# w_down as seven products of 512x512 weight sums, interleaved with w_up, in a one-core hybrid decoder layer

## The chip, the core and the metric

The kernel runs on one core of a Trainium2 chip. The metric is the device time of one execution in microseconds (us), and the figure for the kernel before is the median of three runs. The engines are named as the profile names them: PE (TensorE, matrix products), PEld (its weight loads), DVE (VectorE), ACT (ScalarE), POOL (GpSimd) and SP (SyncE, which here only issues transfers).

## What is computed

One layer on 256 tokens of width 2048, everything in 32-bit floats. The change lies in the last two lines of the layer, with w_up of 2048x8192 and w_down of 8192x2048:

```
h    = RMSNorm(x)
proj = h @ w_in                       # 2048 x 4096, then short convolution, pooling
x    = x + concat(y_conv, y_pool) @ w_out
h    = RMSNorm(x)
u    = relu(h @ w_up)
x    = x + (u * u) @ w_down
out  = RMSNorm(x)
```

## The kernel before

**Products in three parts.** PE multiplies 32-bit numbers here in a reduced form (fp32r). Each operand is split into that form (hi) and what is left of it (lo), and a product is hi·hi + hi·lo + lo·hi. For weights, ACT writes `w_hi` from `w_raw` (L449) and DVE writes `w_lo` = `w_raw` - `w_hi` (L628). For activations the same is done once, and hi and lo lie side by side.

**The stream of weights.** Weights come in chunks of 1 MB, [128 partitions, 4 x 512]: 512 rows by 512 columns of a weight matrix. Four chunks (2048 x 512) are a block. `w_raw`, `w_hi` and `w_lo` have four slots each, one per chunk of a block. SP issues the loads in one order (L197, `load_chunk`) and waits before each until DVE has read the slot four chunks earlier. ACT's `split` waits for the load and until PE has used the slot's previous chunk (`chunk_used`); DVE's `split` waits for ACT. All engines take their instructions strictly in the order written.

**Blocks.** There are 8 blocks of w_in, 4 of w_out, and then four parts p of 4 blocks of w_up and 4 blocks of w_down. Part p of w_up makes 2048 columns of u, and the part's w_down blocks take them up as 2048 rows. Banks of the accumulator (`ps`, 8 banks of 512 columns) are used in two sets of four, in turns.

- An up block (`gemm_block`) makes the transposed values: the weights are stationary, 64 pairs of a matmul of 512 columns (activation hi and lo beside each other, L252) and one of 256 columns (L255). Then ACT copies the one half of the banks to `cross` (L455), DVE adds the other half (`add_halves`, L635), scales by the token's norm (L664), and makes relu and square in one instruction (L891); ACT and DVE split the result into `act_b` (L477, L671).
- A down block (`row_block`, `row_products`, L343) has the activations stationary and the weights moving: 4 chunks x 4 x 3 x 2 token halves = 96 matmuls of 512 columns. DVE adds the two banks to `x` (`add_rows`, L649).

**The end.** The last block runs its two token halves one after the other; while the second runs, the first is normalised; then the second is added (L927), squared and scaled, and stored.

Of the kernel before, what the change touches and what calls it, by code (L numbers as in the profile page):

```python
# [47 lines left out]


def build(nc, x_t, x_rows, w_stream, pool_w, params, g_final, out):  # L50
# [4 lines left out]
    with ctx:  # L55
# [194 lines left out]
        def _(pe):  # L250
# [154 lines left out]
            gemm_block(FIRST_UP + 2, act_a, 0)  # L405
            gemm_block(FIRST_UP + 3, act_a, 1)

            def up_pair(n):
                gemm_block(n, act_a, 0)
                gemm_block(n + 1, act_a, 1)  # L410

            def down_pair(n, acts_before):
                row_block(n, 0, acts_before)
                row_block(n + 1, 1, acts_before)

            with pe.Fori(0, 2) as i:
                down_pair(2 * i + (FIRST_UP + 4), 8)
            with pe.Fori(1, PARTS - 1) as p:
                with pe.Fori(0, 2) as i:
                    up_pair(2 * i + PART_BLOCKS * p + FIRST_UP)  # L420
                with pe.Fori(0, 2) as i:
                    down_pair(2 * i + PART_BLOCKS * p + (FIRST_UP + 4), 4 * p + 8)
# [566 lines left out]
```

## Time and profile before

| | us |
|---|---|
| runs, median of 3 (lowest to highest) | 1001.91 (1000.73 to 1002.18) |
| the profiled execution | 1000.99 |
| its span, first to last instruction | 999.2 |
| PE busy | 986.5 (99%) |
| DVE busy | 586.4 (59%) |
| ACT busy | 419.6 (42%) |
| mean granted TensorE clock | 0.996 |

All durations below are from the one profiled execution. "Span" leaves out 1.8 us of that execution's own time. PE's busy time contains overlaps of pipelined matmuls, so that the pitch from one matmul to the next is read from the chain of waits and not from the duration of one.

### The profile page before, as it was taken

What the parts mean: (1) busy time and instruction counts of PE and PEld (TensorE: products, weight loads), DVE (VectorE), ACT (ScalarE), POOL (GpSimd) and SP (SyncE); (2) the same over time, 40 slices, a digit from 0 to 9 for tenths busy, and PEclk for the clock granted to TensorE, in tenths of its full rate; (3) what the DMA queues carried; (4) which work ended last, traced back from release to release, by engine and by line L of the source; (5) the groups of instructions that cost most, each with busy time, mean ns of one, the idle gap of its engine ahead of it and who ended that gap; (6) DMA issues with size and microseconds to landing.
All of it is one profiled execution on the core that took longest, in us unless ns stands there. A gap on an engine that the chain in (4) does not pass through costs nothing.

```text
span 999.2 us, 12457 instructions
## 1 busy us (share of the span) xinstructions
PE 986.5 (99%) x5088; PEld 847.2 (85%) x5088; DVE 586.4 (59%) x428; ACT 419.6 (42%) x325; POOL 1.4 (0%) x9
## 2 busy tenths in 40 slices
PE   8999999999999999999999999999999999999996
PEld 7888888888888888888888888888888888888885
DVE  6597777655554766544656654556565445656453
ACT  6644435354443434333444433343433334444342
POOL 0000000000000000000000000000000000000000
PEclk9999999999999999999999999999999999999998
DMA  9956543555544655555455455545545554555512
GB/s 327 392 194 229 190 188 122 215 211 190 189 169 169 233 189 195 183 208 177 165 211 206 176 203 191 187 151 213 209 183 207 176 204 132 211 209 205 187 66 84
DMA packets 29694, 193.52 MB, mean 194 GB/s; under 512 B 3296, under 2 KB 3552, under 8 KB 7136
## 3 DMA queue, kind: packets, MB, share of 16 engines
q1 hardware_dynamic: 29232, 190.85, 52.1%
q10 hardware_dynamic: 288, 1.18, 0.3%
q0 software_dynamic: 144, 1.05, 0.3%
q8 instruction: 24, 0.39, 0.2%
q14 instruction: 6, 0.05, 0.0%
HBM read 190.97 MB, written 2.10 MB: 193 GB/s over the span
## 4 chain that ended last, share of the span: by engine, by line
PE 94%; DMA 3%; SPq 1%; DVE 1%; ACT 0%; issue 0%; ACTq 0%
PE ps L343 44%; PE ps L252 33%; PE ps L255 17%; DMA w_raw<-w_stream 3%; SPq L208 1%; PE ps L277 0%; PE ps L329 0%; SPq L193 0%; DVE w_lo L628 0%; ACT w_hi L449 0%; PE ps L317 0%; DVE val L635 0%; PE ps L276 0%; PE ps L279 0%; ACT cross L483 0%
## 5 line engine op out<-in xcount | busy, mean ns | idle before, releaser
L628 DVE TENSOR_TENSOR w_lo<-w_raw,w_hi 128x2048 fp32r<-128x2048 f32 x172 | 392.0, 2291 | 280.4 <-ACT w_hi L449 279.7
L449 ACT ACTIVATE w_hi<-w_raw 128x2048 fp32r<-128x2048 f32 x172 | 326.8, 1912 | 344.0 <-PE ps L343 210.8
L252 PE MATMUL ps<-act_a,w_hi 128*128 128x512 f32 x1472 | 351.1, 391 | 0.0
L343 PE MATMUL ps<-w_hi,act_b 128*128 128x512 f32 x1280 | 345.3, 390 | 0.0
L252 PEld LDWEIGHTS ps<-act_a,w_hi 128*128 128x128 f32 x1472 | 271.0, 188 | 52.5
L343 PEld LDWEIGHTS ps<-w_hi,act_b 128*128 128x128 f32 x1280 | 239.8, 188 | 49.3
L343 PE MATMUL ps<-w_lo,act_b 128*128 128x512 f32 x640 | 199.7, 389 | 0.0
L255 PEld LDWEIGHTS ps<-act_a,w_lo 128*128 128x128 f32 x1472 | 188.6, 191 | 7.0
L255 PE MATMUL ps<-act_a,w_lo 128*128 128x256 f32 x1472 | 191.1, 283 | 0.0
L343 PEld LDWEIGHTS ps<-w_lo,act_b 128*128 128x128 f32 x640 | 120.2, 188 | 25.0
L635 DVE TENSOR_TENSOR val<-ps,cross 128x1024 f32<-128x1024 f32 x26 | 31.8, 1223 | 47.2 <-ACT cross L455 47.2
L455 ACT ACTIVATE cross<-ps 128x1024 f32<-128x1024 f32 x26 | 26.6, 1024 | 76.4 <-PE ps L255 74.6
L477 ACT ACTIVATE act_b<-val 128x1024 fp32r<-128x1024 f32 x18 | 19.1, 1060 | 67.4 <-DVE val L891 59.8
L649 DVE TENSOR_TENSOR x<-ps,x 128x1024 f32<-128x1024 f32 x19 | 23.3, 1224 | 22.4 <-PE ps L343 22.4
L671 DVE TENSOR_TENSOR act_b<-val,act_b 128x1024 fp32r<-128x1024 f32 x18 | 22.1, 1226 | 21.5 <-ACT act_b L477 21.5
L277 PE MATMUL ps<-act_a,w_hi 128*128 128x512 f32 x64 | 23.9, 414 | 2.0 <-DVE w_lo L723 2.0
L664 DVE TENSOR_TENSOR val<-val,inv_rms 128x1024 f32<-128x1024 f32 x18 | 22.0, 1225 | 5.3 <-ACT inv_rms L498 4.7
L483 ACT ACTIVATE cross<-x 128x512 f32<-128x512 f32 x16 | 9.9, 622 | 32.0 <-DVE x L649 18.9
L891 DVE SCALAR_TENSOR_TENSOR val<-val 128x1024 f32<-128x1024 f32 x16 | 19.6, 1226 | 0.6
L279 PE MATMUL ps<-act_a,w_lo 128*128 128x256 f32 x60 | 17.4, 290 | 0.0
L277 PEld LDWEIGHTS ps<-act_a,w_hi 128*128 128x128 f32 x64 | 12.6, 196 | 5.5 <-DVE w_lo L723 2.7
L723 DVE TENSOR_TENSOR w_lo<-w_raw,w_hi 128x512 fp32r<-128x512 f32 x16 | 11.0, 687 | 2.3 <-ACT w_hi L510 2.0
(68 smaller groups left out, 164.3 us busy)
## 6 DMA issues: line engine op xcount, KB each, us to landing
w_raw<-w_stream SPq DMA_DIRECT2D x172, 1024.0 KB, 4.8
w_raw<-w_stream SPq DMA_DIRECT2D x16, 256.0 KB, 7.9
x<-x_rows SPq DMA_DIRECT2D x2, 1024.0 KB, 17.4
mix_mem<-x_t SPq DMA_DIRECT2D x3, 512.0 KB, 8.2
out<-x SPq DMA_DIRECT2D x6, 256.0 KB, 2.7
mix_mem<-pool_w ACTq DMA_DIRECT2D x1, 1024.0 KB, 9.1
mix_mem<-g_final POOLq DMA_DIRECT2D x1, 1024.0 KB, 5.0
out<-val SPq DMA_DIRECT2D x2, 256.0 KB, 2.1
```

Source lines behind the costliest of these rows:

```text
L252: return pe.matmul(ps[:, bank, :], weights_hi, act, start=first, stop=False)
L255: return pe.matmul(ps[:, bank, 0:S], weights_lo, act[:, 0:S], start=False, stop=last)
L277: mm = pe.matmul(ps[:, bank, :], weights_hi, act, start=first, stop=last)
L343: mm = pe.matmul(ps[:, NT * parity + t, :], a[:, at:at + P], cols, start=first and i == 0, stop=last and i == 2)
L449: act.activation(w_hi[:, c, :], w_raw[:, c, :], ACT.Copy).then_inc(hi_ready, 1)
L455: act.activation(cross[:, :, :], bank_halves(parity, 1), ACT.Copy).then_inc(cross_ready, 1)
L628: dve.tensor_tensor(out=w_lo[:, c, :], in0=w_raw[:, c, :], in1=w_hi[:, c, :].bitcast(F32), op=ALU.subtract)\
L635: dve.tensor_tensor(out=val[:, :, :], in0=bank_halves(parity, 0), in1=cross[:, :, :], op=ALU.add).then_inc(summed, 1)
L649: dve.tensor_tensor(out=x_cols(j), in0=row_banks(parity), in1=x_cols(j), op=ALU.add)\
L664: dve.tensor_tensor(out=to, in0=val[:, :, :], in1=by_token(), op=ALU.mult)\
L671: dve.tensor_tensor(out=lo(act_b, k0, k0 + NT), in0=val[:, :, :], in1=hi(act_b, k0, k0 + NT).bitcast(F32), op=ALU.subtract)\
L891: dve.scalar_tensor_tensor(out=val[:, :, :], in0=val[:, :, :], scalar=0.0, in1=val[:, :, :], op0=ALU.max, op1=ALU.mult)\
```

## The change

The 16 up blocks (UPS) stay, one per 512 columns of u. w_down is cut anew: 8 slices (SLICES) of 1024 rows, each in two column halves of 1024, which makes 16 units. A unit is a product of a 256 x 1024 piece A of u·u with a 1024 x 1024 piece B of w_down, each seen as 2 x 2 quadrants (A: token half by 512 columns; B: 512x512, one chunk each).

For 14 units (SEVENS) the four quadrant products of two terms each, eight in all, are replaced by seven products with sums of quadrants (Winograd's variant of Strassen's form). Weight sums: T1 = B11+B12, T2 = T1+B22, T3 = B12+B22, T4 = T2+B21. T1 is made by DVE (a 128x2048 add). T2, T3 and T4 are each made by a transfer that POOL issues with `accum_op=add`, 1 MB from DRAM onto the chunk that lies in the on-chip buffer. The activation sums (S5, N6, N3, S7) are made by DVE on [128, 4, 128] pieces (`made`). Every product goes to one accumulator bank by 12 matmuls of 512 columns (`term`), and DVE adds or subtracts the banks into `x` seven times per unit in instructions of 512 columns (`fold`), reading a bank while it still accumulates for later terms. The two last units are done in the plain way, 8 chunks of 24 matmuls (`plain`).

One unit d is interleaved with one up block t = d+2, in 11 steps: up chunk 0, A11·B11, S5·T1, up chunk 1, N3·B22, N6·T2, up chunk 2, S7·T3, up chunk 3, A12·B21, A22·T4. Two up blocks (LEAD) run ahead. Up blocks always use banks 0 to 3, terms banks 4 to 6. Relu and norm are one DVE instruction (`add_up`) and the square moves to ACT (`square_up`). `w_hi` and `w_lo` keep their four slots, now filled in turn by step number; `w_raw` slots 0 and 1 are for w_up, 2 and 3 for B quadrants, and two more buffers (`sums`, in `mix_mem`) hold T1, T2, T4.

```diff
-            with sp.Fori(2, BLOCKS) as n:
+            with sp.Fori(2, FIRST_UP + LEAD) as n:
                 for c in range(CHUNKS):
                     load_chunk(n, c)
...
+            for t in range(LEAD, UPS):            # SP
+                d = t - LEAD
+                lead = d == 0
+                load_quad(sums[d % 2], d, 1, up_item(1, 0) if d < 2 else term_item(d - 2, A22_T4),
+                          sum_base_loaded[d % 2])
+                load_up(t, 0, up_item(1, 0) if lead else up_item(t - 1, 2))
+                load_quad(w_raw[:, 3, :], d, 3, up_item(1, 3) if lead else term_item(d - 1, S7_T3),
+                          raw_loaded[3])
+                load_up(t, 1, up_item(1, 1) if lead else up_item(t - 1, 3))
+                load_quad(w_raw[:, 2, :], d, 0, up_item(1, 2) if lead else term_item(d - 1, A12_B21),
+                          raw_loaded[2])
+                load_up(t, 2, up_item(t, 0))
+                load_quad(w_raw[:, 2, :], d, 2, term_item(d, A11_B11), raw_loaded[2])
+                load_up(t, 3, up_item(t, 1))
...
+            def add_quad(to, d, n, after, added):        # POOL
+                pool.wait_ge(lo_ready, after + 1)
+                pool.dma_start(to, w_quads[4 * d + n, :, :], accum_op=ALU.add).then_inc(added, 16)
+            for d in range(SEVENS):
+                add_quad(sums[d % 2], d, 3, term_item(d, S5_T1), t2_added)
+                add_quad(w_raw[:, 3, :], d, 1, term_item(d, N3_B22), t3_added)
+                add_quad(sums[d % 2], d, 2, term_item(d, N6_T2), t4_added)
...
+            for t in range(LEAD, UPS):                   # PE
+                d = t - LEAD
+                up_chunk(t, 0)                           # waits: summed by add_up(t - 1)
+                if d == 0:
+                    pe.wait_ge(summed, turn(FIRST_UP) + LEAD)
+                else:
+                    pe.wait_ge(folded, FOLDS * d)
+                term(d, A11_B11, A11, NT, True)
+                term(d, S5_T1, S5, NT + 1, True)
+                up_chunk(t, 1)
+                pe.wait_ge(folded, FOLDS * d + 2)
+                term(d, N3_B22, N3, NT + 1, False)
+                term(d, N6_T2, N6, NT, False)
+                up_chunk(t, 2)
+                pe.wait_ge(folded, FOLDS * d + 4)
+                term(d, S7_T3, S7, NT, False)
+                up_chunk(t, 3)
+                term(d, A12_B21, A12, NT + 2, True)
+                pe.wait_ge(folded, FOLDS * d + 5)
+                term(d, A22_T4, A22, NT, False)
+            pe.wait_ge(quad_ready, quad_count(last_slice, A21))
+            pe.wait_ge(folded, FOLDS * SEVENS - 1)
+            plain(0, range(HALVES), True)
+            pe.wait_ge(folded, FOLDS * SEVENS)
+            plain(1, range(HALVES), True)
...
+            def hi_of(g, raw):                           # ACT
+                act.wait_ge(chunk_used, g - 3)
+                act.activation(w_hi[:, g % 4, :], raw, ACT.Copy).then_inc(hi_ready, 1)
...
+                act.wait_ge(t2_added, 16 * (d + 1))
+                hi_of(term_item(d, N6_T2), sums[d % 2])
...
+                elif not folding:
+                    quad_hi(s + 1, A21, held[:, :, P:S], A22_T4)   # unit 13: waits for its last term
+            plain_hi(0)
+            take_up(UPS - 1)
+            plain_hi(1)
+            square_up(UPS - 1)
...
+            for t in range(LEAD, UPS):                   # DVE, in this order
+                d, s = t - LEAD, (t - LEAD) // 2
+                folding = d % 2 == 0
+                if d:
+                    fold(d - 1, 5, S7_T3, NT, 1, 1, ALU.subtract)
+                if folding:
+                    quad_lo(s, S7, part_2)
+                up_lo(t, 0)
+                add_up(t - 1)
...
+                dve.tensor_tensor(out=sums[d % 2], in0=sums[d % 2], in1=w_raw[:, 2, :], op=ALU.add)\
+                   .then_inc(t1_added, 1)
+                lo_of(term_item(d, A11_B11), w_raw[:, 2, :])
+                dve.wait_ge(squared, t)
+                if folding:
+                    made(... part_0 ...)                 # S5
+                if d:
+                    fold(d - 1, 6, A12_B21, NT + 2, 0, 0, ALU.add)
+                lo_of(term_item(d, S5_T1), sums[d % 2])
+                if folding:
+                    quad_lo(s, S5, part_0)
+                    made(... part_1 ...)                 # N6
+                if d:
+                    fold(d - 1, 7, A22_T4, NT, 1, 0, ALU.add)
+                up_lo(t, 1)
+                if folding:
+                    quad_lo(s, N6, part_1)
+                    made(... part_0 ...)                 # N3
+                elif s + 1 < SLICES - 1:
+                    make_s7()
+                lo_of(term_item(d, N3_B22), w_raw[:, 3, :])
+                if folding:
+                    quad_lo(s, N3, part_0)
+                fold(d, 1, A11_B11, NT, 0, 0, ALU.add)
+                lo_of(term_item(d, N6_T2), sums[d % 2])
+                if folding:
+                    quad_lo(s, A12, val[:, :, 0:P])
+                    quad_lo(s, A22, val[:, :, P:S])
+                else:
+                    quad_lo(s + 1, A11, held[:, :, 0:P])
+                fold(d, 2, S5_T1, NT + 1, 1, 1, ALU.subtract)
+                up_lo(t, 2)
+                lo_of(term_item(d, S7_T3), w_raw[:, 3, :])
+                fold(d, 3, N3_B22, NT + 1, 0, 1, ALU.subtract)
+                up_lo(t, 3)
+                fold(d, 4, N6_T2, NT, 0, 1, ALU.subtract)
+                lo_of(term_item(d, A12_B21), w_raw[:, 2, :])
+                lo_of(term_item(d, A22_T4), sums[d % 2])
+            fold(SEVENS - 1, 5, S7_T3, NT, 1, 1, ALU.subtract)
+            quad_lo(last_slice, A21, held[:, :, P:S])
+            plain_lo(0)
+            add_up(UPS - 1)
+            plain_lo(1)
+            fold(SEVENS - 1, 6, A12_B21, NT + 2, 0, 0, ALU.add)
...
```

`lo_of(g, raw)` waits for `hi_ready` and makes the 128x2048 `w_lo` of step g. `quad_lo` waits for ACT's half of an activation piece, makes the lo part in 512 columns, and waits for its own end; `made` is one 512-column DVE instruction and a wait for its end. `take_up` (ACT) and `add_up` (DVE, an add and the relu-and-norm) stand for L455, L635 and L664/L891. The comments in the diff are added here.

## Rows read from the trace of the kernel before

**Rows 1.** The page's first part: span and busy time by engine.

```profile
span 999.2 us, 12457 instructions
PE 986.5 (99%) x5088; PEld 847.2 (85%) x5088; DVE 586.4 (59%) x428; ACT 419.6 (42%) x325; POOL 1.4 (0%) x9
```

**Rows 2.** The page's chain that ended last: share of the span by line.

```profile
PE ps L343 44%; PE ps L252 33%; PE ps L255 17%; DMA w_raw<-w_stream 3%; SPq L208 1%; PE ps L277 0%; PE ps L329 0%; SPq L193 0%; DVE w_lo L628 0%; ACT w_hi L449 0%; PE ps L317 0%; DVE val L635 0%; PE ps L276 0%; PE ps L279 0%; ACT cross L483 0%
```

**Rows 3.** The chain in order of time: start us, us, what.

```profile
285.28 3.63 PE ps L252 x16
...
551.77 87.07 PE ps L343 x384
638.84 3.63 PE ps L252 x16
...
727.87 87.07 PE ps L343 x384
```

**Rows 4.** Waits: engine line waited for, us in total, times, longest us.

```profile
DVE w_lo L628 <- ACT w_hi L449: 279.7, 134, 7.0
```

**Rows 5.** Groups by line and shape: count | busy, mean ns | idle before, releaser.

```profile
L628 DVE TENSOR_TENSOR w_lo<-w_raw,w_hi 128x2048 fp32r<-128x2048 f32 x172 | 392.0, 2291 | 280.4 <-ACT w_hi L449 279.7
L449 ACT ACTIVATE w_hi<-w_raw 128x2048 fp32r<-128x2048 f32 x172 | 326.8, 1912 | 344.0 <-PE ps L343 210.8 <-PE ps L255 129.0 <-DMA w_raw<-w_stream 4.1
L635 DVE TENSOR_TENSOR val<-ps,cross 128x1024 f32<-128x1024 f32 x26 | 31.8, 1223 | 47.2 <-ACT cross L455 47.2
L455 ACT ACTIVATE cross<-ps 128x1024 f32<-128x1024 f32 x26 | 26.6, 1024 | 76.4 <-PE ps L255 74.6 <-PE ps L277 1.8
L527 ACT ACTIVATE act_b<-win 128x512 fp32r<-128x512 f32 x4 | 2.5, 633 | 20.9 <-DVE win L760 20.9
L927 DVE TENSOR_TENSOR x<-ps,x 128x512 f32<-128x512 f32 x2 | 1.4, 690 | 10.1 <-PE ps L343 10.1
```

**Rows 6.** DVE in order of time: start us, us, what; the starts give the pitch.

```profile
103.14 1.23 DVE L664 TENSOR_TENSOR mix_mem<-val,inv_rms 128x1024 f32<-128x1024 f32 x1
104.40 1.22 DVE L809 TENSOR_TENSOR mix_mem<-mix_mem,inv_rms 128x1024 f32<-128x1024 f32 x1
105.55 2.29 DVE L628 TENSOR_TENSOR w_lo<-w_raw,w_hi 128x2048 fp32r<-128x2048 f32 x1
107.75 0.69 DVE L749 TENSOR_TENSOR win<-mix_mem 128x512 f32<-128x512 f32 x1
108.47 2.15 DVE L749 TENSOR_TENSOR win<-win 128x512 f32<-128x512 f32 x3
```

**Rows 7.** Busy time in two stretches: PE, PEld, DVE, ACT, POOL, PEclk, DMA share, GB/s.

```profile
639.00:727.00 88.00, 88.00 (x507) 77.74 (x506) 52.20 (x29) 36.21 (x22) 0.00 (x0) 1.00 0.51 190
12.00:41.00 29.00, 29.00 (x164) 25.37 (x164) 17.77 (x28) 21.14 (x32) 0.15 (x1) 1.00 1.03 415
```

**Rows 8.** Transfers: count, KB each, median us from issue to landing; POOL's one issue.

```profile
w_raw<-w_stream SPq DMA_DIRECT2D x172, 1024.0 KB, 4.8
x<-x_rows SPq DMA_DIRECT2D x2, 1024.0 KB, 17.4
mix_mem<-g_final POOLq DMA_DIRECT2D x1, 1024.0 KB, 5.0
...
200.58 0.65 POOL L246 DMA_DIRECT2D mix_mem<-g_final  x1 [146.98 <-DVE val L842]
```

**Rows 9.** Stretches of 1 us around two idle times of PE, columns as in rows 7.

```profile
6.00:7.00 1.00, 0.00 (x0) 0.00 (x0) 0.24 (x1) 0.63 (x1) 0.00 (x0) 1.00 0.84 200
...
8.00:9.00 1.00, 1.00 (x5) 0.90 (x4) 0.48 (x1) 0.15 (x2) 0.00 (x0) 0.50 0.98 361
...
10.00:11.00 1.00, 1.00 (x4) 0.57 (x3) 1.00 (x3) 1.00 (x3) 0.00 (x0) 0.50 1.01 397
...
991.00:992.00 1.00, 0.05 (x1) 0.00 (x0) 0.88 (x2) 0.19 (x1) 0.00 (x0) 1.00 0.00 0
...
994.00:995.00 1.00, 0.00 (x0) 0.00 (x0) 0.96 (x3) 0.86 (x2) 0.00 (x0) 0.54 0.00 0
```

More of the change, by code:

```diff
@@ L404, in _ @@
             pe.wait_ge(inv_rms_ready, 2)
[L405 to L422, printed above, removed]
@@ new lines, in plain @@
+            def plain(f, halves, done):
+                g = FIRST_PLAIN + f
+                d, k2, n = PLAIN_OF[f]
+                bank = (6, 4, 0, 2)[2 * d + n]
+                of_half = ((A11, A21), (A12, A22))[k2]
+                pe.wait_ge(hi_ready, g + 1)
+                pe.wait_ge(lo_ready, g + 1)
+                for k in range(CK):
+                    for i, (at, of) in enumerate(((0, w_hi), (P, w_hi), (0, w_lo))):
+                        for t in halves:
+                            mm = pe.matmul(ps[:, bank + t, :], quads[:, of_half[t], k, at:at + P],
+                                           weights_of(of, g, k), start=k2 == 0 and k == 0 and i == 0,
+                                           stop=k2 == 1 and k == CK - 1 and i == 2)
+                if done:
+                    mm.then_inc(chunk_used, 1)
+                return mm
@@ L440, in _ @@
+            plain(5, range(HALVES), True)
+            for t in range(HALVES):
+                plain(6, (t,), False)
+                plain(7, (t,), False).then_inc(half_done, 1)
         @block.scalar
@@ new lines, in plain_hi @@
+            def plain_hi(f):
+                slot, loads = plain_raw(f)
+                act.wait_ge(raw_loaded[slot], 16 * (loads + 1))
+                hi_of(FIRST_PLAIN + f, w_raw[:, slot, :])
+            plain_hi(0)
+            take_up(UPS - 1)
+            plain_hi(1)
+            square_up(UPS - 1)
+            act.wait_ge(squared, UPS)
+            quad_hi(SLICES - 1, A12, val[:, :, 0:P], A12_B21)
+            quad_hi(SLICES - 1, A22, val[:, :, P:S], A22_T4)
+            for f in range(2, PLAINS):
+                plain_hi(f)
@@ new lines, in _ @@
+            plain_lo(0)
+            add_up(UPS - 1)
+            plain_lo(1)
+            fold(SEVENS - 1, 6, A12_B21, NT + 2, 0, 0, ALU.add)
+            dve.wait_ge(squared, UPS)
+            quad_lo(last_slice, A12, val[:, :, 0:P])
+            quad_lo(last_slice, A22, val[:, :, P:S])
+            plain_lo(2)
+            fold(SEVENS - 1, 7, A22_T4, NT, 1, 0, ALU.add)
+            plain_lo(3)
+            plain_lo(4)
+            plain_lo(5)
+            dve.wait_ge(folded, FOLDS * SEVENS)
```

312 lines of the change are left out of this document (244 added, 68 removed).

## The prediction

> **What bounds the kernel now.** The page's head comes first: PE is busy for 986.5 of 999.2 us, DVE for 586.4, ACT for 419.6 [rows 1]. The chain that ended last shows whether that is work or overlap: L343, L252 and L255 hold 94% of the span, transfers 3% [rows 2]. In order of time the chain has whole blocks without a gap: 384 matmuls of L343 in 87.07 us, which is 0.2268 us each, and then up blocks from 638.84 to 727.87, which is 89.03 us for 16 chunks, 5.56 each [rows 3]. The waits say the same from the other side: DVE's longest total is for ACT (279.7 us), and ACT in its turn waits for slots that PE frees [rows 4, 5]. In a stretch of up blocks DVE is busy for 52.2 of 88 us at a clock of 1.00 and a DMA share of 0.51 [rows 7]. PE is the bound and is fed in time; only fewer PE columns make the kernel faster, as long as DVE, whose work grows most, keeps up.
>
> **What goes from PE.** Eight quadrant products of 12 matmuls become seven in 14 units: 14 x 12 = 168 matmuls of 512 columns fewer, x 0.2268 = **-38.1 us** [rows 3]. A unit with its up block is then 4 x 5.56 + 7 x 2.72 = 41.3 us of PE, against 44.0 before.
>
> **What DVE gets, and where.** Prices by pitch (start to start) [rows 6]: a 128x2048 instruction 2.20 (105.55 to 107.75); 1024 columns 1.26 if the next waits for its end (103.14 to 104.40), else 1.15; 512 columns 0.72 with such a wait (107.75 to 108.47), else 0.62 (0.69 less the same overlap of 0.07). A fold is the shape of L927, 0.69 us [rows 5]. Per unit: 11 `lo_of` and T1, 12 x 2.20 = 26.4; `add_up` 2.4; 7 folds 4.3; in even units nine pieces of activation sums 6.5, in odd ones two, 1.4. That makes 39.6 us (even) and 34.5 (odd) out of 41.3. It fits as a sum, 90% busy, but DVE goes in one fixed order and PE waits in the middle of it, so the order decides.
>
> I follow one even unit from T, the moment PE ends S7·T3 of the unit before. Two things fix DVE's start: up chunk 3 ends at T+5.56, ACT's copy takes 1.02 [rows 5], so `add_up` begins at T+6.6 whatever DVE did before (until then it has lo A22·T4, a fold, a piece and lo of up chunk 0, done at about T+5). From there to the end of fold 2 stand: add and scale 2.41; six 128x2048 instructions (T1 and lo of A11·B11, S5·T1, up chunk 1, N3·B22, N6·T2) 13.2; three `made` and five `quad_lo` 5.76; folds 6, 7, 1 and 2 2.55. Sum 23.9, end T+30.6. PE may start N3·B22 only after fold 2 (`folded` 7d+2). Without waits it would be there at T + 3 x 5.56 + 4 x 2.72 = T+27.6. So PE stands for **3.0 us in each even unit**, even if no transfer is late. In an odd unit six pieces less give T+26.2, 1.3 us to spare. After fold 2 nothing is late: fold 4 ends at T+38.5, S7·T3 needs it at T+41.6. DVE's next start is fixed again by up chunk 3, so a period is the end of fold 2 plus 13.7 us of PE, and no stall is won back. ACT is no bound: 11 x 1.91 + 2 x 1.02 + at most 7 x 0.63 = 27.5 us of 41.
>
> **The accumulating transfer.** T2 is sent by POOL after lo of S5·T1 (T+17.1 even, T+16.4 odd). ACT's hi (1.91) and DVE's lo (2.29) of N6·T2, then two or one `quad_lo` and fold 2, stand behind its landing: fold 2 ends at T+23.4+L even, T+22.0+L odd, L from DVE's end to the landing. It hurts above L = 7.2 (even) and 5.6 (odd). The queue behind that waiting ACT instruction holds the activation pieces, up chunk 2 and S7·T3; behind DVE's lo stands the fold that PE waits for. No row shows an accumulating transfer. Lower bound: POOL's plain 1 MB, 5.0 us [rows 8]; upper: 17.4 us, a 1 MB load queued behind the first rush [rows 8]. I take L = 8.0: the issue 0.65, the plain landing 4.8 [rows 8], and once more the bytes, since the sum must read what it adds to: 1.05 MB at the 415 GB/s of the busiest stretch is 2.5 us [rows 7]. That lies nearer the row of 5.0, as these transfers meet one or two others and not a dozen. It gives a wait of 3.8 us in even units and 2.4 in odd ones. T3 (9 us until needed) and T4 (13 us) pass at that L. Were L 5.0, even units wait 3.0 and odd ones not at all; at 17.4 they wait 13.2 and 11.8.
>
> The Trainium skill (Collectives: The Full Stack, "The bandwidth ceiling: the fold count and why AG ≠ RS ≠ AR") says that a transfer with an add emits two source reads per chunk into the same ring, so that it delivers about half of a copy's rate. No row here shows it. By that rule the data part of L is doubled, which is my 8.0; by a copy's price L would be 5.5 and the sum 23 us lower.
>
> **The first unit** has no terms of a unit before it, so PE comes earlier. With E the end of the second up block, `add_up` starts at E+1.1; T1, two lo's, a `made` and `quad_lo` of S5 end at E+11.5, where PE wanted S5·T1 at E+8.3: 3.2 us. Then fold 2 ends at 10.9 + 8.0 + 6.3 = E+25.2 and PE is there at E+19.8: 5.4 us. Together 8.6 (7.2 at the low L).
>
> **The tail.** Activation piece A21 of the last slice waits on ACT for the last term of unit 13, although its slot holds nothing; call that moment X. ACT: piece to X+0.6, hi of plain 0 to X+2.5, copy of the last up block to X+3.5. DVE: lo of plain 0 from X+2.5, `add_up` (2.4), lo of plain 1, fold 6. PE's plain 0 waits for fold 6: 2.5 + 2.20 + 2.41 + 2.20 + 0.69 = **10.0 us** during which PE has nothing. After that plain 1 (5.44 us later) finds fold 7 done, and the end (L927 and on) is as before.
>
> **The clock.** PE was idle throughout 6 to 7 us; the granted clock was 0.50 (1.2 GHz) at 8 to 9 and still at 10 to 11 us. At the end PE stops 0.05 us after 991; the clock is 1.00 there and 0.54 at 994 to 995 [rows 9]. So a stop of some 3 us lets it fall, and three us at half speed cost 1.5. The tail and the first unit pay it: 3.0. The six other even stops of 3.8 us are just beyond 3: between 0 and 1.5 each, I take 0.75, the middle: 4.5. Odd units: none.
>
> **Sum.** -38.1 + 8.6 + 6 x 3.8 + 7 x 2.4 + 10.0 + 3.0 + 4.5 = +27.6. The profiled execution took 1000.99 us with its ends (span 999.2); 1000.99 + 27.6 = 1028.6. The median of the runs is 0.9 above the profiled one: **1029 us**. The likeliest case's own range, L from 6.5 to 9.5 and the clock at either bound, is 1008 to 1055.
>
> **Rivals.**
> 1. *The transfer costs what a plain one does* (L up to 5.6). Then only DVE's order binds: 7.2 + 6 x 3.0 + 10.0 = 35.2, clock 3.0 to 7.5: with -38.1 that is +0.1 to +4.6 on 1001.9, so 1002 to 1007. For it: POOL's plain transfer landed in 5.0 us. Against it: the buffer must be read too, and odd units send T2 only 2.8 us before two plain loads follow.
> 2. *Faster: the order has more slack than counted.* The place is fold 2 in even units. If DVE reaches it 3 us earlier (from which point the stop is gone) and L is below 5.6, only the first unit and the tail are left: -38.1 + 7.2 + 10.0 + 3.0 = -17.9, 984 us. For it: DVE's sum of 39.6 fits in 41.3. Against it: add_up's start hangs on PE's up chunk 3, and each instruction behind it is priced by its own pitch.
> 3. *Transfers crowd each other.* A unit moves 8 plain chunks and 3 accumulating ones; counted double that is 14.7 MB, 35 us at 415 GB/s in a period of 45, against a DMA share of 0.51 now [rows 7]. With L = 11, even units wait 6.8, odd ones 5.4, the first 11.6, and the clock falls in nearly all: -38.1 + 11.6 + 40.8 + 37.8 + 10.0 + 14 x 1.5 + 1.5 = +84.6, 1087 us. For it: the row of 17.4. Against it: the median of 4.8 with half the engines' time free.
> 4. *The change doesn't do what it says*, for instance if the matmuls of `term` come at another pitch than 0.2268. They have the operands' shapes of L343, so this gets little.
>
> **Chances.** Forecast 0.43, rival 1 0.17, rival 2 0.22, rival 3 0.15, rival 4 0.03. A measurement of this kernel can tell 0.2% (2 us) from no change. Faster: rival 2 and a little of 1, 0.25. Same: the low part of rival 1, 0.08. Slower 0.67. The range for 8 in 10 cuts rival 3 above a mean L of about 10, and half of rival 2: 984 to 1062.
>
> **What would show it.** Matmuls of 512 columns fewer by 168. In the middle of every even unit a gap of PE ahead of N3·B22, released by DVE's fold, of 3 to 4 us; in odd units one of about 2.4 behind `t2_added`. ACT's hi of N6·T2 waiting for the transfer; its landing near 7.3 us after the issue. A gap of 10 us after the last term, clock 0.5 behind it. DVE busy near 88%. The forecast is wrong if PE has no gaps in even units (then DVE's order was read wrong), if the landing is below 5 us, or if waits stand at up chunks, behind plain loads.

## The result: 1059.5 us, 5.9% slower

| | before | after | forecast |
|---|---|---|---|
| median of 4 runs each (lowest to highest), us | 1001.32 (1000.36 to 1002.18) | 1059.46 (1058.86 to 1062.32) | 1029 (984 to 1062) |
| ratio to before, 95% interval | 1 | 1.0587 (1.0564 to 1.0609) | |
| profiled execution / its span, us | 1000.99 / 999.2 | 1059.1 / 1057.2 | 1028.6 |
| mean granted TensorE clock | 0.996 | 0.966 | |

The direction was right, the size was not: +58.1 us between the profiled executions, +27.6 forecast. The page of after, first part, the chain by engine and the transfers (they answer to [rows 1, 2, 8]):

```profile
span 1057.2 us, 12002 instructions
PE 982.4 (93%) x4920; PEld 835.2 (79%) x4920; DVE 765.4 (72%) x619; ACT 525.9 (50%) x420; POOL 37.7 (4%) x51
...
PE 56%; DVE 18%; DMA 14%; issue 6%; ACT 4%; SPq 1%; ACTq 0%; DVEq 0%
...
w_raw<-w_quads SPq DMA_DIRECT2D x50, 1024.0 KB, 5.6
mix_mem<-w_quads POOLq DMA_DIRECT2D x28, 1024.0 KB, 10.1
...
w_raw<-w_quads POOLq DMA_DIRECT2D x14, 1024.0 KB, 11.2
```

PE has the 168 matmuls less. But where 94% of the chain of before was matmuls, PE now holds 56%, and DVE, transfers and ACT hold 36%: PE is fed too late. The two lines of POOL are the adding transfers: 10.1 us (T2 and T4) and 11.2 us (T3) from issue to landing.

**An odd unit**, the chain in order of time from the end of up chunk 3 on (start us, us, what; it answers to [rows 3]), and PE's own row (the bracket is the idle time before it and its releaser):

```profile
377.46 1.03 ACT cross L772
...
378.51 1.23 DVE win L1148
...
380.91 2.29 DVE mix_mem L1198
383.20 2.01 DVE w_lo L1138
...
386.00 2.21 DVE w_lo L1138
...
388.50 8.71 DMA mix_mem<-w_quads
...
397.23 1.93 ACT w_hi L758
...
401.39 0.69 DVE act_b L1157
402.10 0.70 DVE x L1167
...
402.85 0.50 PE ps L546
```

```profile
402.85 0.50 PE L546 MATMUL ps<-w_hi,act_b 128*128 128x512 f32 x1 [2.72 <-DVE x L1167]
```

Read it downwards: copy, `add_up`, T1 (L1198), lo of A11·B11, lo of S5·T1 (L1138), then POOL's T2, which lands 9.0 us after DVE's end (388.21 to 397.21), hi and lo of N6·T2, an activation piece, fold 2 (L1167), and PE starts N3·B22 2.72 us late. That is the chain which the prediction followed, link by link.

**The clock behind the stop.** Four stretches of 1 us behind that stop, columns as in [rows 7]:

```profile
403.00:404.00 1.00, 1.00 (x5) 0.83 (x6) 1.00 (x1) 0.00 (x0) 0.00 (x0) 1.00 0.97 262
404.00:405.00 1.00, 1.00 (x5) 0.76 (x4) 0.99 (x1) 0.00 (x0) 0.00 (x0) 0.61 1.06 270
405.00:406.00 1.00, 1.00 (x4) 0.81 (x3) 0.00 (x0) 0.00 (x0) 0.00 (x0) 0.50 0.81 197
406.00:407.00 1.00, 1.00 (x4) 0.71 (x4) 0.00 (x0) 0.41 (x1) 0.00 (x0) 0.50 1.30 262
```

The granted clock falls from 1.00 to 0.50 (2.4 to 1.2 GHz), 1.4 us after PE has restarted at 402.85, and matmuls of 512 columns start 0.43 us apart instead of 0.23 until it comes back.

**An even unit** ends by another chain, in order of time, and has a stop of its own (PE's row below it):

```profile
534.57 2.30 DVE w_lo L1138
...
537.16 10.19 DMA w_raw<-w_quads
...
547.37 1.93 ACT w_hi L758
...
549.35 2.17 issue
551.53 0.68 DVE x L1167
...
552.27 2.06 issue
554.33 0.69 DVE x L1167
...
555.06 0.50 PE ps L546
```

```profile
437.65 0.50 PE L546 MATMUL ps<-w_hi,act_b 128*128 128x512 f32 x1 [2.61 <-DVE x L1167]
```

T3 lands 10.2 us after its issue; hi, then DVE's lo of S7·T3 and of up chunk 3 (both "issue" here), with fold 3 between them and fold 4 behind, and PE gets S7·T3. The stop of 2.61 us stands ahead of A11·B11, where PE waits for `folded` 7d, fold 7 of the unit before; its odd-unit twin is 0.43 us.

**The balance.** Stops are PE's idle time in the trace; half clock is the sum of 1 minus the granted clock over stretches of 1 us in which it was below 0.95.

| | stops, us | half clock, us | sum | forecast |
|---|---|---|---|---|
| first unit | 0.63 + 2.33 + 4.53 = 7.5 | 3.4 | 10.9 | 8.6 + 1.5 |
| 6 even units, each | 2.61 + 0.64 = 3.25 | 1.7 | 4.95 | 3.8 + 0.75 |
| 7 odd units, each | 0.43 + 3.12 = 3.55 | 1.95 | 5.5 | 2.4 + 0 |
| tail | 10.15 | 2.8 | 12.95 | 10.0 + 1.5 |

All stops in the units sum to 51.9 us (forecast 8.6 + 22.8 + 16.8 = 48.2), the half clock in them to 27.2 (forecast 6.0). With -38.1 and both figures of the tail that is 54.0 of 58.1 us. In the tail the clock is at 0.50 when PE restarts at 1002.74 and stays there for 5.6 us, of which this stretch shows five:

```profile
1003.00:1008.00 5.00, 5.00 (x13) 3.89 (x12) 4.91 (x5) 2.71 (x2) 0.00 (x0) 0.50 0.77 234
```

The rest, 4.1 us, fits the way in which stops are counted. The up chunk ahead of the stop of 2.61 us runs from 429.34 to 437.65, 8.31 us where 5.54 is usual: a delay of 2.77, 0.16 more than the idle time, because the profile draws a matmul 0.39 us long when the next one starts after 0.23. For the 29 stops that makes about 4.6 us.

### The profile page after: what moved, and what is told of

Its sections match the earlier page's. It is cut to its first block, busy times and chain, and to the rows that moved or that the text cites. A ratio compares the mean times of both kernels' runs of the same rounds, so it can differ in the third digit from the quotient of the medians.

```text
span 1057.2 us, 12002 instructions
## 1 busy us (share of the span) xinstructions
PE 982.4 (93%) x4920; PEld 835.2 (79%) x4920; DVE 765.4 (72%) x619; ACT 525.9 (50%) x420; POOL 37.7 (4%) x51
## 4 chain that ended last, share of the span: by engine, by line
PE 56%; DVE 18%; DMA 14%; issue 6%; ACT 4%; SPq 1%; ACTq 0%; DVEq 0%
PE ps L364 20%; PE ps L367 11%; DVE w_lo L1138 8%; PE ps L455 8%; DMA mix_mem<-w_quads 8%; PE ps L588 4%; PE ps L546 4%; DMA w_raw<-w_quads 4%; PE ps L548 4%; PE ps L552 4%; ACT w_hi L758 3%; DVE mix_mem L1198 2%; DMA w_raw<-w_stream 2%; DVE x L1167 2%; ACT cross L772 1%
## 5 line engine op out<-in xcount | busy, mean ns | idle before, releaser
L364 PE MATMUL ps<-act_a,w_hi 128*128 128x512 f32 x1472 | 349.8, 390 | 0.0
L1138 DVE TENSOR_TENSOR w_lo<-w_raw,w_hi 128x2048 fp32r<-128x2048 f32 x120 | 274.3, 2287 | 60.6 <-ACT w_hi L758 59.4
L546 PE MATMUL ps<-w_hi,act_b 128*128 128x512 f32 x392 | 167.4, 427 | 51.3 <-DVE x L1167 48.9
L367 PE MATMUL ps<-act_a,w_lo 128*128 128x256 f32 x1472 | 191.0, 283 | 0.0
L548 PE MATMUL ps<-w_hi,act_b 128*128 128x512 f32 x392 | 164.3, 419 | 0.0
L758 ACT ACTIVATE w_hi<-mix_mem 128x2048 fp32r<-128x2048 f32 x42 | 80.6, 1918 | 123.5 <-DMA mix_mem<-w_quads 69.5
L1138 DVE TENSOR_TENSOR w_lo<-mix_mem,w_hi 128x2048 fp32r<-128x2048 f32 x42 | 96.1, 2288 | 60.5 <-ACT w_hi L758 60.3
L546 PEld LDWEIGHTS ps<-w_hi,act_b 128*128 128x128 f32 x392 | 79.8, 204 | 73.4 <-DVE x L1167 54.6
L552 PE MATMUL ps<-w_lo,act_b 128*128 128x512 f32 x392 | 110.6, 406 | 0.6 <-DVE w_lo L1138 0.6
L552 PEld LDWEIGHTS ps<-w_lo,act_b 128*128 128x128 f32 x392 | 78.4, 200 | 18.6 <-DVE w_lo L1138 1.1
L548 PEld LDWEIGHTS ps<-w_hi,act_b 128*128 128x128 f32 x392 | 80.0, 204 | 16.1
L455 PE MATMUL ps<-w_hi,act_b 128*128 128x512 f32 x256 | 68.8, 390 | 0.0
L1167 DVE TENSOR_TENSOR x<-x,ps 128x512 f32<-128x512 f32 x98 | 66.8, 681 | 1.1
L455 PEld LDWEIGHTS ps<-w_hi,act_b 128*128 128x128 f32 x256 | 47.8, 188 | 9.7
L351 POOL DMA_DIRECT2D mix_mem<-w_quads x28 | 24.3, 868 | 795.0 <-DVE w_lo L1138 795.0
L588 PE MATMUL ps<-w_hi,act_b 128*128 128x512 f32 x128 | 37.5, 407 | 10.2 <-DVE x L1167 10.2
## 6 DMA issues: line engine op xcount, KB each, us to landing
mix_mem<-w_quads POOLq DMA_DIRECT2D x28, 1024.0 KB, 10.1
mix_mem<-w_quads SPq DMA_DIRECT2D x14, 1024.0 KB, 12.9
w_raw<-w_quads POOLq DMA_DIRECT2D x14, 1024.0 KB, 11.2
```

Of the source, the lines that this page charges most:

```text
L364: return pe.matmul(ps[:, bank, :], weights_hi, act, start=first, stop=False)
L367: return pe.matmul(ps[:, bank, 0:S], weights_lo, act[:, 0:S], start=False, stop=last)
L455: mm = pe.matmul(ps[:, NT * parity + t, :], a[:, at:at + P], cols, start=first and i == 0, stop=last and i == 2)
L546: pe.matmul(to, quads[:, quad, k, 0:P], weights_of(w_hi, g, k), start=first and k == 0, stop=False, skip_group_check=not first)
L548: pe.matmul(to, quads[:, quad, k, P:2 * P], weights_of(w_hi, g, k), start=False, stop=False, skip_group_check=not first)
L552: mm = pe.matmul(to, quads[:, quad, k, 0:P], weights_of(w_lo, g, k), start=False, stop=k == CK - 1, skip_group_check=not first)
```

## The experiments

All ratios are to before, timed on the same chip (its medians there 1000.3 to 1000.8 us). Where an expectation names theories by letter, A is the late landing of the adding transfers (A1: by their own double reading), C the plain loads that they crowd. "Unit" is the time from one ACT copy of an up block to the next, even and odd as the parity of d.

### The adding transfer by itself

A small kernel in which POOL sends the same 1 MB transfer in four ways: copies one by one, adding ones one by one, four at once, and adding ones beside SP's plain loads.

> A small kernel that holds only transfers of 1 MB (128 x 2048 floats) from DRAM, issued by POOL, one after the other: six copies, six adding ones onto the same buffer, four copies at once, four adding ones at once, and six adding ones beside a stream of copies from SP. The rest of the layer is left out and the output is zeros. Theory A1 (an adding transfer moves its bytes twice): copies land in 5.0 to 5.6 us, adding ones in 7.5 to 8.1; four at once take about 12 and 22 us. Theory A2 (adding is slower than twice the bytes, whatever is beside it): adding ones land in 9 to 10 us alone. Beside the stream: over 10 us by either.

POOL in order of time (the bracket: idle before, and what it waited for):

```profile
22.89 0.53 POOL L26 DMA_DIRECT2D buf<-w  x1 [4.81 <-DMA buf<-w]
...
50.10 0.86 POOL L29 DMA_DIRECT2D buf<-w  x1 [7.40 <-DMA buf<-w]
58.34 0.85 POOL L29 DMA_DIRECT2D buf<-w  x1 [7.38 <-DMA buf<-w]
...
82.80 2.13 POOL L32 DMA_DIRECT2D buf<-w  x4 [7.39 <-DMA buf<-w]
95.91 3.57 POOL L36 DMA_DIRECT2D buf<-w  x4 [10.98 <-DMA buf<-w]
118.85 3.51 POOL L39 MEMSET zero<- 128x4096 f32 x1 [19.37 <-DMA buf<-w]
...
148.81 0.87 POOL L42 DMA_DIRECT2D buf<-w  x1 [12.08 <-DMA buf<-w]
161.01 0.86 POOL L42 DMA_DIRECT2D buf<-w  x1 [11.34 <-DMA buf<-w]
```

One after the other, a copy takes 5.34 us (17.55 to 22.89) and an adding transfer 8.24 (50.10 to 58.34). Four at once take 13.1 us as copies (82.80 to 95.91) and 22.9 as adding ones (95.91 to 118.85), 1.75 times as long. Beside a stream of plain loads one takes 12.2. So the estimate of 8.0 was right for a transfer alone, and wrong for one in company. The rule of the Trainium skill that the prediction weighed (Collectives: The Full Stack, "The bandwidth ceiling: the fold count and why AG ≠ RS ≠ AR"), a transfer with an add at about half a copy's rate, is what the group of four shows within an eighth.

### The transfers' price in the kernel

> POOL's three transfers of each unit are plain 1 MB copies instead of adding ones (T2, T3 and T4 are then not sums); every instruction, wait and order stays. Theory A (the landing of the adding transfer sets the end of 14 units, since it is longer than a copy's): in the changed kernel it landed 9.0 us (odd units) and 10.5 us (even units) after DVE's instruction; a copy should land in 5.5 to 6.5 us. Odd units then take about 41.5 to 42 us, even ones 45.4 us (fold order and the clock), so 14 units shrink from 657 to about 610 us and the kernel takes about 1012 us. Rival B (the order of DVE's instructions alone makes the time, the transfer lies beside it): over 1045 us.

```diff
-pool.dma_start(to, w_quads[4 * d + n, :, :], accum_op=ALU.add).then_inc(added, 16)
+pool.dma_start(to, w_quads[4 * d + n, :, :]).then_inc(added, 16)
```

1011.82 us (1010.91 to 1013.33), ratio 1.0110 (1.0094 to 1.0127). The transfers of its page:

```profile
mix_mem<-w_quads POOLq DMA_DIRECT2D x28, 1024.0 KB, 5.3
...
w_raw<-w_quads POOLq DMA_DIRECT2D x14, 1024.0 KB, 6.7
```

Without the add 48 of the 58 us are gone. The units are 42.0 to 42.4 us (odd) and 44.6 to 45.8 (even): the fold-2 stop is gone from both, which leaves 0.43 us in odd units, and in even ones the 2.61 ahead of A11·B11 with the clock behind it.

> POOL's three transfers of each unit are left out, and ACT doesn't wait for them (T2, T3, T4 are never formed). Theory A: only DVE's order, the first unit and the tail are left: 1005 to 1012 us, within 6 us of the run with plain copies. Rival C (crowding: the plain loads of SP are late because the adding transfers share the engines with them): clearly faster than the run with plain copies, by 10 us or more. Rival B: over 1045 us.

```diff
-add_quad(sums[d % 2], d, 3, term_item(d, S5_T1), t2_added)      # and those of T3 and T4
-act.wait_ge(t2_added, 16 * (d + 1))                             # and those for T3 and T4
```

1012.36 us (1011.89 to 1014.29), ratio 1.0117 (1.0100 to 1.0134). The same as with copies, so moving 42 MB more beside the loads costs nothing. In after itself, all 29 waits of ACT for a transfer in the units end with the landing of an adding one and none with a plain load; crowded plain loads are no cause there. The add's landing is.

### The order in which DVE meets a late landing

> Only DVE's order is changed: fold 2 goes ahead of lo of N6T2, folds 3 and 4 go ahead of lo of S7T3. PE waits for these folds, and they no longer stand behind an instruction that waits for an adding transfer. The transfers stay as they are. Theory A, second part (the landing costs time only because the folds stand behind it in DVE's order): PE needs hi of N6T2 at T+30 and has it at T+27, so odd units take 41.7 us and even ones 45.4 (the stop ahead of A11B11 and the clock remain): about 1012 us, as with plain copies. If PE itself waits for the sums (the landing is exposed in any order), the time stays above 1045 us.

```diff
 fold(d, 1, A11_B11, NT, 0, 0, ALU.add)
+fold(d, 2, S5_T1, NT + 1, 1, 1, ALU.subtract)
 lo_of(term_item(d, N6_T2), sums[d % 2])
...
+fold(d, 3, N3_B22, NT + 1, 0, 1, ALU.subtract)
+fold(d, 4, N6_T2, NT, 0, 1, ALU.subtract)
 lo_of(term_item(d, S7_T3), w_raw[:, 3, :])
-fold(d, 3, N3_B22, NT + 1, 0, 1, ALU.subtract)
 up_lo(t, 3)
-fold(d, 4, N6_T2, NT, 0, 1, ALU.subtract)
```

1023.98 us (1022.08 to 1028.14), ratio 1.0229 (1.0212 to 1.0246): 35 us back with the transfers still landing in 10.2 and 12.3 us. Odd units are 42.0 again; a landing of 10 us costs nothing there, and it cost 5 us only because folds that need no transfer stood behind a `lo_of` that waits for one. The time is 12 us above the expected 1012 all the same. Even units stay at 47.2 to 49.2, where 45.4 was expected: DVE still waits at lo of S7·T3, is late at fold 7, and the stop ahead of A11·B11 grows from 2.6 to between 4.0 and 4.8 us.

> Only fold 7 of the unit before is moved ahead of the first activation sum, so that the stop of 2.6 us ahead of A11B11 in even units goes. Theory A: no gain to speak of, since the chain through T3's transfer ends later than that stop: 1053 to 1060 us; the 2.6 us come back as a longer wait ahead of N3B22 or S7T3. Rival B (stops of DVE's order add up): 6 x 2.6 us and the clock less, 1035 to 1040 us.

```diff
+fold(d - 1, 6, A12_B21, NT + 2, 0, 0, ALU.add)
+fold(d - 1, 7, A22_T4, NT, 1, 0, ALU.add)
 made(... part_0 ...)                                  # S5
-fold(d - 1, 6, A12_B21, NT + 2, 0, 0, ALU.add)
 lo_of(term_item(d, S5_T1), sums[d % 2])
...
-fold(d - 1, 7, A22_T4, NT, 1, 0, ALU.add)
```

A miss: 1081.86 us (1079.78 to 1084.22), ratio 1.0807 (1.0789 to 1.0825), 22 us slower than after. PE in order of time:

```profile
453.07 0.80 PE L546 MATMUL ps<-w_hi,act_b 128*128 128x512 f32 x1 [5.48 <-DVE x L1167]
...
456.65 1.91 PE L552 MATMUL ps<-w_lo,act_b 128*128 128x512 f32 x4
```

The stop of 2.61 us is gone from A11·B11, but DVE's chain to fold 2 is no shorter: PE comes earlier and waits there in one piece (4.3 to 7.1 us in all units but the first). In the unit of these rows the clock is already at half in the first matmul after it (0.80 us) and stays there for 5.9 us, now behind the stop where it delays what follows. POOL's T2 goes out 0.8 us later, because fold 7 now stands ahead of lo of S5·T1. An early stop was cover for a late one.

> Only the end of the stretch is changed: ACT's piece A21 no longer waits for the last term of unit 13, and DVE does folds 6 and 7 of that unit ahead of lo of plain 1 and add_up. By the prediction's tail (10.0 us of waiting, measured 10.15, and half clock behind it) the kernel gets 10 to 11.7 us faster: 1047 to 1050 us. If the wait only moves to the next chunk of weights, under 5 us.

```diff
-quad_hi(s + 1, A21, held[:, :, P:S], A22_T4)
+quad_hi(s + 1, A21, held[:, :, P:S], None)            # no wait for the last term
...
 plain_lo(0)
-add_up(UPS - 1)
+fold(SEVENS - 1, 6, A12_B21, NT + 2, 0, 0, ALU.add)
+fold(SEVENS - 1, 7, A22_T4, NT, 1, 0, ALU.add)
 plain_lo(1)
-fold(SEVENS - 1, 6, A12_B21, NT + 2, 0, 0, ALU.add)
+add_up(UPS - 1)
```

1045.49 us (1044.24 to 1046.65), ratio 1.0443 (1.0425 to 1.0460), 14.0 less than after and 1.5 more than was expected at most. Between the profiled executions it is 12.5 (1059.1 and 1046.65): 9.1 of the stop, of which 1.07 us are left, and 2.8 of the clock behind it. The change removes this row of after, the forecast's tail of 10.0 us:

```profile
1002.74 1.20 PE L588 MATMUL ps<-w_hi,act_b 128*128 128x512 f32 x2 [10.15 <-DVE x L1167]
```

> The adding transfers stay as they are; the order on DVE is mended in all places that the traces point to: T1 is added ahead of add_up (in DVE's idle time), folds 6 and 7 follow lo of A11B11, fold 2 goes ahead of lo of N6T2, folds 3 and 4 ahead of lo of S7T3, and the tail as in the run of the tail alone. Theory A (latency exposed by order, not by bandwidth): PE waits only in the first unit and for DVE's work of 39.6 us now and then: 14 x 41.6 us, 970 to 985 us, faster than the kernel before. If DVE at 90% load can't keep up beside its waits for ACT and the transfers: 990 to 1005 us. If the engines that move data are the bound: over 1010 us.

The three orders above, and:

```diff
+dve.tensor_tensor(out=sums[d % 2], in0=sums[d % 2], in1=w_raw[:, 2, :], op=ALU.add)   # T1, with its waits
 add_up(t - 1)
-dve.tensor_tensor(out=sums[d % 2], in0=sums[d % 2], in1=w_raw[:, 2, :], op=ALU.add)
```

A miss again: 1022.29 us (1020.12 to 1026.15), ratio 1.0218 (1.0189 to 1.0246), where 970 to 985 was expected. DVE's row of T1, and the chain's row ahead of it:

```profile
508.96 2.29 DVE L1197 TENSOR_TENSOR mix_mem<-mix_mem,w_raw 128x2048 f32<-128x2048 f32 x1 [0.28 <-DMA w_raw<-w_quads]
```

```profile
502.19 6.74 DMA w_raw<-w_quads
```

B11 lands 6.74 us after lo of A12·B21 has let its slot go; T1 waits for it and takes 2.2 us, and `add_up`, which PE needs at up chunk 0, stands behind both (stops of 1.4 to 3.6 us there). The same orders without that move:

> As the run with all orders mended, but T1 is added behind add_up again, as in the changed kernel. There T1, moved ahead, waited for the load of B11 (6.7 to 8.4 us after lo of A12B21) and held add_up and so PE's next up chunk back by 1.4 to 3.6 us in each unit. Theory D (that wait took what the other orders gave): PE is not held at the up chunks any more, 14 x 2.4 us less 1 or 2: 992 to 1005 us. If the adding transfer of T3 (12 us) is the bound by itself: 1012 us or more.

1004.50 us (1002.87 to 1007.53), ratio 1.0046 (1.0030 to 1.0061), clock 0.994, just inside the expected 992 to 1005: 55 of the 58 us are given back by orders alone, and this still does not reach before. In this order ACT does wait for a plain load, too. In each unit but the first, its first hi (A11·B11) stands 2.8 to 4.8 us for the load of B11, for instance:

```profile
506.78 1.92 ACT L758 ACTIVATE w_hi<-w_raw 128x2048 fp32r<-128x2048 f32 x1 [3.21 <-DMA w_raw<-w_quads]
```

> The run with orders mended, without POOL's transfers and ACT's waits for them (T2, T3, T4 are never formed). What is left is PE's columns and the order of DVE: 14 x 41.5 to 42 us, first unit 3 to 4 us late: 968 to 978 us. It bounds what any faster way of making the weight sums could reach; if it stays above 990 us, DVE's load is what the mended orders lack and not the transfers.

```profile
span 966.2 us, 11938 instructions
PE 950.9 (98%) x4920; PEld 816.6 (85%) x4920; DVE 766.5 (79%) x619; ACT 527.5 (55%) x420; POOL 1.4 (0%) x9
```

968.14 us (967.55 to 969.20), ratio 0.9681 (0.9665 to 0.9697). With the same orders and no sums by transfer, every unit but the first (40.9) is 41.3 to 41.4 us, the forecast's 41.3 of PE. So DVE's load is no bound in a right order, and the adding transfers cost 36 us even then. How much of that is their own landing, and how much the loads of B11 that are late beside them, is not separated: plain copies were not run in this order.

### The clock

> PE does eight matmuls of 512 columns into an unused bank (1.8 us, their result is not read) at the places where it stops: ahead of the wait for fold 2 in odd units, and ahead of the wait before A11B11 in even units. Everything else is as in the changed kernel. If the half clock behind the stops is on the path in odd units (1.5 us each) it goes, since the remaining idle time is about 1 us: 7 x 1.5 = 10 us faster, 1048 us; in even units nothing is gained, as T3's transfer ends later. If the clock doesn't matter, 1058 to 1062 us.

```diff
+for _ in range(8):                        # odd units; in even ones ahead of the wait for 7d
+    pe.matmul(ps[:, 7, :], act_a[:, 0, 0:P], act_a[:, 1, :], start=True, stop=True)
 pe.wait_ge(folded, FOLDS * d + 2)
```

1051.86 us (1050.92 to 1055.07), ratio 1.0521 (1.0504 to 1.0539), 7.6 less than after. The half clock in the units shrinks from 27.2 to 6.7 us, so only a third of it came back. Odd units in which it no longer fell take 45.5 to 46.4 us, the two in which it did 47.9 and 48.0: there it is on the path. Even units hardly move (46.3 for 46.7), since T3's chain ends them whatever PE's clock does before: with fillers as without, S7·T3 starts within 0.2 us of the end of fold 4.

### Company of the transfers

> The changed kernel with the loads of w_up in the 14 units cut to 64 of 2048 columns (the rest of w_up is left out, old values are multiplied in its place); every instruction and wait stays. Theory A with crowding (the adding transfer takes 8.2 us alone and 9 to 12 beside other loads): T2 and T3 land in 8.3 to 9 us, 14 units get 1.0 to 1.5 us shorter each: 1036 to 1046 us. If the plain loads beside them don't matter: over 1055 us.

```diff
-sp.dma_start(w_raw[:, c % 2, :], w_stream[CHUNKS * (FIRST_UP + t) + c, :, :])
+sp.dma_start(w_raw[:, c % 2, 0:64], w_stream[CHUNKS * (FIRST_UP + t) + c, :, 0:64])
```

1046.61 us (1045.81 to 1047.75), ratio 1.0466 (1.0448 to 1.0483), 12.9 less than after, 0.6 above the upper end of what was expected. Odd units take 45.3 us for 47.1, even ones 46.5 for 46.7. Landings:

```profile
mix_mem<-w_quads POOLq DMA_DIRECT2D x28, 1024.0 KB, 8.6
...
w_raw<-w_quads POOLq DMA_DIRECT2D x14, 1024.0 KB, 10.3
```

> The changed kernel with the loads of w_up in the 14 units cut to 64 of 2048 columns and T4's transfer and its wait left out (both leave part of w_up and w_down out of the result), order and everything else kept, so that the adding transfers of T2 and T3 have nearly no company. Landing then 8.2 to 8.6 us for both, as in the run of transfers alone. Theory A with its parts sized: odd units 16.4 + 8.5 + 5.6 + 13.7 and 1.5 for the clock = 45.6 us; even ones 45.4 by DVE's order and the clock behind the stop ahead of A11B11: 1034 to 1042 us, which leaves about 8 to 12 us over the forecast of 1029 for the clock in odd units. If it falls to 1029 or below, crowding was the whole of what the forecast missed.

The same without T4: 1045.17 us (1041.73 to 1047.68), ratio 1.0444 (1.0415 to 1.0472).

```profile
mix_mem<-w_quads POOLq DMA_DIRECT2D x14, 1024.0 KB, 8.1
...
w_raw<-w_quads POOLq DMA_DIRECT2D x14, 1024.0 KB, 10.1
```

T2 lands as in the small kernel, and the first odd unit, in which the clock stays at 1.00, takes 44.3 us (forecast 43.7); from the next one on the clock falls and odd units take 46.2 on average. T3's median stays at 10.1 us, but it still has company: SP's 1 MB load of the base of a later T1 (B12 into `mix_mem`), issued some 3 us before it. In even units the two are in flight together for 3.4 to 4.5 us and T3 takes 8.5 to 10.2, in odd ones for 5.8 to 8.5 us and it takes 10.4 to 11.6. Unit 13 has no such load. T3's issues in units 11 and 13:

```profile
w_raw<-w_quads POOLq DMA_DIRECT2D x1, 1024.0 KB, 10.4
...
w_raw<-w_quads POOLq DMA_DIRECT2D x1, 1024.0 KB, 8.1
```

The run before has 8.2 us in unit 13, too. That points to this load; no run leaves it out alone.

> As the run before in this list, and POOL waits for the landing of T3's transfer before it issues T4's. T3's and T4's adding transfers were in flight together (issues 4 us apart), and T3, which is needed first, landed after 12 us. Theory E (the adding transfers crowd each other): T3 lands in 9.5 to 10.5 us and the kernel gets 5 to 15 us faster than without this. Against it: T4 lands later and may hold hi of A22T4: no gain, or a loss.

On top of the mended orders:

```diff
+pool.wait_ge(t3_added, 16 * (d + 1))
 add_quad(sums[d % 2], d, 2, term_item(d, N6_T2), t4_added)
```

1046.14 us (1042.75 to 1046.25), ratio 1.0447 (1.0428 to 1.0465), 42 slower than the orders alone. POOL's wait (us in total, times, longest):

```profile
POOL mix_mem L351 <- DMA w_raw<-w_quads: 161.8, 14, 12.5
```

POOL's queue is in order too: T4 and the next T2 leave late. T3 still landed in 12.2 us, so T4 was not what slowed it.

### Looking for a version that beats before

Five more kernels move the sums about within the mended orders. N3·B22's operands first, T3 so being sent earlier, with T4 still later (it inherits that fault):

> As the run with T4 later, and in even units hi and lo of N3B22 go ahead of the activation sums N6 and N3 on ACT and DVE, so that T3's transfer is issued 2.1 us earlier. If T3's transfer is the end of a unit's chain, even units get up to 2 us shorter: 6 to 14 us faster than without. If DVE's load of 39.6 us is the bound: no difference beyond 2 us. Best guess 985 to 998 us, below the kernel before.

1049.39 us (1043.86 to 1051.84), ratio 1.0483 (1.0445 to 1.0521). Without it:

> The run with orders mended (T1 behind add_up, all sums by transfer, 1004.5 us) with N3B22 ahead in even units. The same reasoning: 992 to 998 us if T3's transfer ends even units there.

```diff
-quad_hi(s, N6, part_1, N6_T2)
 hi_of(term_item(d, N3_B22), w_raw[:, 3, :])
+quad_hi(s, N6, part_1, N6_T2)                         # DVE: lo of N3·B22 ahead of made(N6)
```

1002.56 us (1000.70 to 1004.95), ratio 1.0023 (1.0013 to 1.0033). T2 by a DVE add of the size of T1's, in all units, and in odd ones only:

> The run with orders mended (T1 behind add_up), and T2 = T1 + B22 is added by DVE right after lo of S5T1 in all units (2.2 us more of DVE each: 41.8 us in even units, 36.7 in odd ones), so that POOL only issues T3 and T4. Theory F (in that run the serial chain of T2's and T4's transfers on one buffer ends odd units, and T3's even ones): odd units near 41.6 us, even ones 43 to 45: 985 to 998 us. If DVE's load is the bound: 14 x (39.3 + waits), over 1003 us.

> The same with T2 added by DVE in odd units only, by a transfer in even ones. Theory F: odd units near 41.6 us, even ones as in the run with orders mended (44): 985 to 993 us, faster than with T2 by DVE in all units by 0 to 10 us, since DVE's 2.2 us ahead of lo of N3B22 delay T3's transfer there. If both are equal, T3's transfer is no longer what ends even units.

```diff
-add_quad(sums[d % 2], d, 3, term_item(d, S5_T1), t2_added)
...
 lo_of(term_item(d, S5_T1), sums[d % 2])
+dve.tensor_tensor(out=sums[d % 2], in0=sums[d % 2], in1=w_raw[:, 3, :], op=ALU.add).then_inc(t2_by_dve, 1)
```

1008.24 us (1007.23 to 1009.28), ratio 1.0079 (1.0062 to 1.0096), and 1001.62 us (1000.00 to 1004.27), ratio 1.0011 (1.0002 to 1.0021). In the first, odd units are 41.3 to 43.2 but even ones 46.0 to 47.1. There the added instruction stands between lo of S5·T1 and lo of the piece S5, and PE stops 2.7 us ahead of S5·T1 (0.5 with all sums by transfer):

```profile
522.18 0.57 PE L546 MATMUL ps<-w_hi,act_b 128*128 128x512 f32 x1 [2.69 <-DVE act_b L1157]
```

A place behind that piece was not tried. N3 first with T2 by DVE in odd units:

> The run with T2 by DVE in odd units, and in even units hi and lo of N3B22 go ahead of the activation sums N6 and N3, so that T3's transfer is issued 2.1 us earlier. In the run before even units took 45.0 us and odd ones 43.0, with PE waiting for hi of S7T3 in even units. If T3's transfer ends even units: 43 us instead of 45, 986 to 993 us, the first version below the kernel before. If DVE's work does: within 3 us of 1002.

1000.75 us (997.56 to 1003.04), ratio 1.0003 (0.9993 to 1.0013). All five best guesses were too low, the first by 51 us, the others by 5 to 10; two times fit the other branch that was named, DVE's load or work as the bound (over 1003 with T2 by DVE in all units, within 3 us of 1002 in the last). Even the last has units of 42.3 to 45.0 us behind the first, not 41.3. PE stops in its even units 1.2, 0.5 and 0.9 us, each time for DVE, and transfers still hold 26% of its chain; which of the two binds is not separated. The best of them equals before; none that forms all the sums beats it.

## Why the prediction went wrong, point by point

The direction and the chain were right; what failed is mainly one term, the clock. The forecast was 30.5 us short (+58.1 against +27.6). Half clock in the units was 27.2 us where 6.0 was forecast, and 13.6 of these 21 us lie in the odd units, where the term stood at nothing.

- **What goes from PE: right.** 168 matmuls fewer, and 41.3 us for a unit that waits for nothing.
- **DVE's load: right.** 39.6 and 34.6 us per unit, as forecast (39.6, 34.5). Two unit stretches of after, columns as in [rows 7]:

```profile
422.10:469.10 47.00, 43.48 (x214) 36.71 (x213) 39.61 (x30) 25.43 (x18) 2.58 (x3) 0.96 0.81 246
469.10:515.50 46.40, 43.43 (x215) 36.75 (x214) 34.62 (x25) 23.67 (x15) 2.59 (x3) 0.96 0.82 249
```

- **The clock: this term failed.** The forecast gave even stops 0.75 us each and odd ones none, because it took "a stop of some 3 us" as the point from which the clock falls. Behind nearly all stops of 2.5 to 2.9 us it fell too, for 1.7 us of PE time each. The tail's clock was 2.8 for 1.5. In odd units it lies on the path (3.4 us per unit missed: about 1.9 of it clock); in even units most of it is cover for T3's chain, as the filled stops showed.
- **L: right alone, too low in company.** 8.2 us by itself; in the kernel, from DVE's end and on average, 8.5 for T2 in even units, 9.4 in odd ones, and 11.0 for T3 in even units. Without most of the company (no T4, small loads of w_up) odd units take 1.3 us less (45.86 for 47.13), some of it clock, and even ones 0.7 less (45.96 for 46.69).
- **"T3 passes": failed.** It ends every even unit. Hi, two lo's and two folds stand between its landing and PE, and T3 can't be sent before lo of N3·B22, which itself comes late. At 11.0, where the forecast had 9 us until it was needed, there was no slack left.
- **The place of the even stop: half failed.** The wait for fold 7 ahead of A11·B11 was not in my walk. It takes 2.61 us. Only 0.40 on average are left at fold 2, where the forecast had all of it, and 0.24 stand ahead of S7·T3. The sum, 3.25, is near the forecast 3.8, and it hangs on the same DVE chain: with fold 7 moved ahead, PE waited for fold 2 instead.
- **First unit and tail: their stops right**, 7.5 (8.6) and 10.15 (10.0), both with a dearer clock (3.4 and 2.8 for 1.5 each).
- **Rivals.** Rival 1's price is the kernel with plain copies, 1012 and not 1002 to 1007: its clock, too, was underrated. Rival 2's slack exists only in another order and without landings (968). Rival 3 had the right mechanism too large: T2's L in odd units rose to 9.4, not 11. Its clock, 1.5 us in nearly every unit, was nearer to what was measured (1.7 and 1.95) than the forecast's.

The runs show that the add's landings cost 48 us (the plain copies), and that most of it came through what DVE and PE have queued behind them (the folds first, the mended orders). Open are what the last 36 us in the mended order are made of, and whether the sums can be formed fast enough at all; the 32 us between before and the mended orders without transfers are there only if they can.

## What to carry to other kernels

Price a late landing by what stands behind the instruction that waits for it, on every in-order queue: put work that needs no transfer ahead of it, and check what the moved work itself waits for (T1, POOL's T4). A stop is not only its own length; count the clock behind it, and ask whether it covers another stop that will come out when it is removed. A kernel without the disputed part altogether, in the best order, tells early what the whole idea can give.

## What the runs showed of the hardware

- An adding transfer of 1 MB into the on-chip buffer takes 8.2 us against 5.3 for a copy, 1.75 times as long in a group of four, and 12.2 beside a stream of plain loads. Its issue holds POOL for 0.86 us against 0.53.
- Stops as short as 1.94 us (small loads of w_up) were followed by a clock of 0.50, and the length of one stop doesn't tell what it costs. With small loads and no T4 one of 2.06 us had nothing behind it, the next odd unit's of 2.03 a half clock of 1.7. In after, of the six stops of 2.6 us in even units one had none behind it, four 1.7 and one 3.4 us; odd stops of 3.86 and 4.35 us had 3.4 and 1.7.
